# Half of the modulation product's weight loads on VectorE instead of TensorE, and a last tile finished bank by bank

## What is computed

```python
c_act = jax.nn.silu(c)                       # (1, 2048)
for l in range(2):
    mod = c_act @ w_mod[l] + b_mod[l]        # w_mod[l]: (2048, 6144)
    shift, scale, gate = jnp.split(mod, 3, axis=-1)
    h = rmsnorm(x, norm_gain[l]) * (1.0 + scale[:, None, :]) + shift[:, None, :]
    proj = h @ w_in[l]
    ...                                      # attention, retention: y
    x = x + gate[:, None, :] * (y @ w_out[l])
...
# PEER, for each token t: 8 heads x 16 chosen experts
a = gelu(einsum('thkd,td->thk', u[idx], hb))
out = einsum('thk,thkd->td', g * a, v[idx])  # added to the residual, then stored
```

## Time and profile before

| | us |
|---|---|
| median of 3 runs | 3162.84 (3162.42 to 3167.22) |
| the profiled execution's own time | 3161.82 |
| its span, first to last instruction | 3159.6 |
| PE busy (share of the span) | 2164.9 (69%) |
| DVE busy | 1692.1 (54%) |
| ACT busy | 853.3 (27%) |
| DMA, mean rate | 285 GB/s |

### The profile page before, as it was taken

How to read it: one execution, slowest core, us unless ns; L and a number is a source line. 1 busy time by engine, 2 the same in 40 slices (tenths; PEclk the granted TensorE clock), 3 DMA queues, 4 the chain that set the end, 5 groups by cost and what they waited for, 6 DMA issues and landing times.

```text
span 3159.6 us, 30717 instructions
## 1 busy us (share of the span) xinstructions
PE 2164.9 (69%) x12338; PEld 1487.2 (47%) x12338; DVE 1692.1 (54%) x2583; ACT 853.3 (27%) x1267; POOL 806.4 (26%) x680
## 2 busy tenths in 40 slices
PE   5899999989999999999989973223222222322335
PEld 2666677877778787667668872000000000000001
DVE  3436556654756664343335688665565555565430
ACT  1333443443444454454545421000000000000000
POOL 1111100000000000000000026665555555555552
PEclk8999999999999999999989987665666666666667
DMA  9888865557665555343325689999999999999998
GB/s 385 285 294 271 287 213 153 181 166 243 207 190 157 152 178 158 116 134 106 107 86 162 207 323 406 422 422 421 422 421 422 421 422 420 422 421 422 421 422 338
DMA packets 243593, 901.00 MB, mean 285 GB/s; under 512 B 20374, under 2 KB 45228, under 8 KB 177004
## 3 DMA queue, kind: packets, MB, share of 16 engines
q0 software_dynamic: 94208, 612.85, 48.3%
q1 hardware_dynamic: 148768, 285.58, 27.9%
q10 hardware_dynamic: 476, 0.62, 0.1%
HBM read 894.78 MB, written 2.10 MB: 284 GB/s over the span
## 4 chain that ended last, share of the span: by engine, by line
PE 56%; DMA 30%; DVE 7%; ACT 3%; issue 2%; POOL 2%; SPq 0%; DVEq 0%; ACTq 0%; POOLq 0%
PE pp L1786 48%; DMA late<-in_peer_v,MI 9%; PE tp L1786 6%; DMA P<-in_peer_v,MI 5%; DMA x<-in_peer_v,MI 5%; DMA ring<-in_peer_v,MI 4%; DMA SY<-in_peer_v,MI 2%; DVE wL L1112 2%; PE tp L1789 2%; DMA late<-in_w_mod 2%; ACT wH L613 1%; DMA ring<-in_peer_w_query 1%; POOL late L2319 1%; DMA ring<-in_w_in 1%; DMA P<-in_w_mod 0%
## 5 line engine op out<-in xcount | busy, mean ns | idle before, releaser
L1112 DVE TENSOR_TENSOR wL<-ring,wH 128x1024 fp32r<-128x1024 f32 (+3 forms) x504 | 583.8, 1162 | 765.0 <-ACT wH L613 763.7
L1786 PE MATMUL pp<-wH,hH 128*128 128x512 f32 (+3 forms) x1888 | 747.8, 396 | 16.2 <-issue 7.9
L613 ACT ACTIVATE wH<-ring 128x1024 fp32r<-128x1024 f32 (+3 forms) x504 | 508.0, 1010 | 784.8 <-PE pp L1786 650.8
L1786 PE MATMUL pp<-wH,hL 128*128 128x512 f32 (+3 forms) x1888 | 718.3, 380 | 0.0
L1786 PE MATMUL pp<-wL,hH 128*128 128x512 f32 (+3 forms) x1888 | 717.7, 380 | 0.0
L1786 PE MATMUL pp<-late,S 128*32 128x512 f32 x768 | 234.5, 892 | 336.9 <-DMA x<-in_peer_v,MI 157.9
L1786 PEld LDWEIGHTS pp<-wH,hH 128*128 128x128 f32 x1888 | 360.0, 191 | 159.5 <-issue 90.6
L1786 PEld LDWEIGHTS pp<-wH,hL 128*128 128x128 f32 x1888 | 359.2, 190 | 63.6
L1786 PEld LDWEIGHTS pp<-wL,hH 128*128 128x128 f32 x1888 | 360.8, 191 | 56.1 <-issue 1.0
L1745 DVE CUSTOM_DVE_ANT_0 late<-late,P 128x2048 f32<-128x2048 f32 x84 | 191.3, 2288 | 154.0 <-DMA late<-in_peer_u,MI 153.8
L1786 PE MATMUL pp<-P,S 128*32 128x512 f32 x360 | 157.8, 873 | 166.8 <-DMA late<-in_peer_v,MI 91.4
(11 more groups left out here) (303 smaller groups left out, 2925.5 us busy)
## 6 DMA issues: line engine op xcount, KB each, us to landing
ring<-in_w_in SPq DMA_DIRECT2D x288, 512.0 KB, 4.0
ring<-in_w_out SPq DMA_DIRECT2D x96, 512.0 KB, 4.4
P<-in_w_mod POOLq DMA_DIRECT2D x85, 512.0 KB, 4.9
late<-in_w_mod SPq DMA_DIRECT2D x64, 512.0 KB, 9.4
SY<-in_w_mod POOLq DMA_DIRECT2D x43, 512.0 KB, 5.1
ring<-in_w_in SPq DMA_DIRECT2D x48, 368.0 KB, 4.6
ring<-in_peer_w_query SPq DMA_DIRECT2D x32, 512.0 KB, 7.2
ring<-in_w_in SPq DMA_DIRECT2D x24, 344.0 KB, 3.2
```

What stands on the lines that cost most here:

```text
L613: act(heads(wH[k % NB][:, 0:2 * wd], 2), raw, ACT.Copy).then_inc(*tick("act_hi", ("hi", k)))
L1112: tt(lo, raw, hi.bitcast(F32), ALU.subtract).then_inc(*tick("dve_lo", *names))
L1786: return e.matmul(o, l, r, start=start, stop=stop, skip_group_check=skip)
```

## The change

From block 4 on, only the even k of a block are taken by PE. For the odd k, DVE multiplies the load by the column of `cact` and sums it into an accumulator of 128 x 1024 in four parts (`mod_acc`: 512 columns in hM, 256 in msum, 256 in U) with three instructions: 512, 256 and 256 columns. After k = 15, in a lane step of its own, PE waits for DVE's sums and adds the accumulator over its partitions with four more matmuls, whose weights are ones. A block has 17 lane steps instead of 16. The loads, their three buffers and their issuer stay as they were, but an odd load's buffer is now freed by DVE.

At the end of a token tile each bank has its own mark (`summed`), DVE adds a bank when that bank is done, and SP and ACT store its 512 columns with two DMAs each: 16 DMAs of 32 rows x 512 columns on either queue in the whole program, where SP had 8 of 32 x 2048.

```diff
@@ sync, add; scalar has the same with (2, 3), "out_act_done"
+            def store_rows(t, parts, sem):
+                for d in range(4):
+                    w.wait_ge(*at("added", t, d))
+                    for q in parts:
+                        e.dma_start(rows_d[t, 32 * q:32 * q + 32, d * 512:(d + 1) * 512],
+                                    xP[q:128:4, t, d * 512:(d + 1) * 512]).then_inc(*landed(sem, ("out", t, d, q)))
...
-                    w.wait_ge(*at("added", t, 3))
-                    for q in range(4):
-                        e.dma_start(rows_d[t, 32 * q:32 * q + 32, :], P[q:128:4, 0, t * D:(t + 1) * D]).then_inc(
-                            *landed("out_done", ("out", t, q)))
+                    store_rows(t, (0, 1), "out_done")
@@ scalar, store
-                                w.wait_ge(*at("mod used", 191 if p else 159))
+                                for m in (189, 190, 191) if p else (157, 158, 159):
+                                    w.wait_ge(*at("mod used", m))
@@ vector, mods
                     for k in range(16):
-                        if k < 15:
+                        if block >= 4 and k % 2:
+                            m = 16 * block + k
+                            w.wait_ge(*at("mod", m))
+                            w.wait_ge(*now("dve_side"))
+                            if k == 1 and block > 4:
+                                w.wait_ge(*at("side", block - 1))
+                            for o, acc in ((0, mod_acc_01), (512, mod_acc[2]), (768, mod_acc[3])):
+                                wv = mod_in[mod_slot(m)[0]][:, o:o + acc.shape[1]]
+                                names = [("mod used", m)] + ([("mod sums", block)] if k == 15 else []) if o == 768 else []
+                                if k == 1:
+                                    ts(acc, wv, cact[:, k:k + 1], None, ALU.mult, None).then_inc(*tick("dve_side", *names))
+                                else:
+                                    stt(acc, wv, cact[:, k:k + 1], acc, ALU.mult, ALU.add).then_inc(*tick("dve_side", *names))
+                        if k < 15 or block >= 4:
                             yield
@@ vector, add
-                    w.wait_ge(*at("mixed", 4 * t + 3, 7))
                     for d in range(4):
+                        w.wait_ge(*at("summed", t, d))
                         v = xP[:, t, d * 512:(d + 1) * 512]
                         tt(v, v, pp[d][:, :], ALU.add).then_inc(*tick("dve_h", ("added", t, d)))
@@ tensor, mods
-                        w.wait_ge(*at("mod", m))
+                        if block < 4 or k % 2 == 0:
+                            w.wait_ge(*at("mod", m))
+                            for g in range(4):
+                                z = mm(side_bank[32 * g:32 * g + 32, 0:256], cact[:, k:k + 1].to_broadcast([128, 32]),
+                                       wv[:, 256 * g:256 * g + 256], k == 0, k == 15)
+                            z.then_inc(*tick("pe_side", ("mod used", m), *([("side", n)] if k == 15 else [])))
+                        if k < 15 or block >= 4:
+                            yield
+                    if block >= 4:
+                        w.wait_ge(*at("mod sums", block))
                         for g in range(4):
...
+                            z = mm(side_bank[32 * g:32 * g + 32, 0:256], ones[:, 0:32], mod_acc[g], False, True)
+                        z.then_inc(*tick("pe_side", ("side", n)))
```

More of the change, by code:

```diff
@@ L422, in mixer_peer_program @@
                      "dve_lo", "dve_stored", "dve_x", "dve_y", "dve_h", "dve_side",
-                     *[f"mod_in{i}" for i in range(11)], "const_in", "pos_in", "x_in", "meta_in", "forget_in", "ffn_in", "decay_in", "turned_in", "out_done",
+                     *[f"mod_in{i}" for i in range(11)], "const_in", "pos_in", "x_in", "meta_in", "forget_in", "ffn_in", "decay_in", "turned_in", "out_done", "out_act_done",
                      *[f"ring_in{i}" for i in range(NS)], *[f"expert_in{i}" for i in range(NG)]):
@@ L456, in mixer_peer_program @@
                   SY[:, 1536:2560]]
+        mod_acc_01 = hM.rearrange("p k n -> p (k n)")
+        mod_acc = mod_acc_01[:, 0:256], mod_acc_01[:, 256:512], msum[:, 256:512], U[:, 3840:4096]
         bf, bf_s = sm[:, 72:80], sm[:, 80:88]
@@ L566, in mods @@
                             *landed(f"mod_in{b}", ("mod", m)))
-                for m in range(16 * b0, 16 * b1):
+                for m in range(16 * b0, 16 * b1 + (b1 - b0 if b0 else 0)):
                     yield
@@ L597, in sync, with store_rows @@
                     lanes.drain(*a)
-            w.wait_ge(*at("out", 1, 3))
+            w.wait_ge(*at("out", 1, 3, 1))
+            w.wait_ge(*at("out", 1, 3, 3))
         def scalar(e, w):
             act = e.activation
+            def store_rows(t, parts, sem):
+                for d in range(4):
+                    w.wait_ge(*at("added", t, d))
+                    for q in parts:
+                        e.dma_start(rows_d[t, 32 * q:32 * q + 32, d * 512:(d + 1) * 512],
+                                    xP[q:128:4, t, d * 512:(d + 1) * 512]).then_inc(*landed(sem, ("out", t, d, q)))
             turn, side, loads, cut = itertools.count(), itertools.count(), itertools.count(), itertools.count()
@@ L1068, in scalar @@
                     act(sc[i % 2], tp[u % 2][:, 0:512], ACT.Copy, scale=rsd[:, 4 + i // 4:5 + i // 4]).then_inc(*tick("act_h", ("pair free", u), ("scores", i)))
+                elif what == "add":
+                    store_rows(a[0], (2, 3), "out_act_done")
                 elif what == "gelu":
@@ L1893, in mods @@
                                 w.wait_ge(*at("side out", n - 1))
-                        w.wait_ge(*at("mod", m))
-                        for g in range(4):
[L1896 to L1900, removed]
+                        if block < 4 or k % 2 == 0:
[4 more added lines that the diff above has]
+                            z.then_inc(*tick("pe_side", ("mod used", m), *([("side", n)] if k == 15 else [])))
+                        if k < 15 or block >= 4:
+                            yield
+                    if block >= 4:
+                        w.wait_ge(*at("mod sums", block))
+                        for g in range(4):
+                            z = mm(side_bank[32 * g:32 * g + 32, 0:256], ones[:, 0:32], mod_acc[g], False, True)
+                        z.then_inc(*tick("pe_side", ("side", n)))
                     yield
@@ L2290, in tensor @@
                             if d == 3:
-                                m.then_inc(*tick("pe_piece", ("expert used", n), *([("mixed", i, b)] if c == 3 else [])))
+                                m.then_inc(*tick("pe_piece", ("expert used", n), *([("mixed", i, b)] if c == 3 else []),
+                                                 *([("summed", i // 4, d)] if final and c == 3 else [])))
+                            elif final and c == 3:
+                                m.then_inc(*tick("pe_piece", ("summed", i // 4, d)))
                 elif what == "open":
@@ L2341, in mods @@
                     yield
+                    if b0 and m % 16 == 15:
+                        yield
             def meta_sum(p, n):
```

## The result

| | before | after |
|---|---|---|
| median, us | 3162.84 (3162.42 to 3167.22) | 3185.6 (3177.06 to 3191.49) |
| ratio, 95% interval | | 1.0069 (1.0056 to 1.0082) |
| profiled execution's own time | 3161.8 | 3184.4 |
| span | 3159.6 | 3182.5 |

What follows compares the result with a forecast made beforehand. PE was taken to bind from 124 to about 950 us, the gathers from 1800 us on; -28.9 - 10.9 + 14.4 + 34 + 5 - 2.5 = +11.1 us gave 3173 us, forecast 3164 to 3184, range 3147 to 3190.

Steps and rivals of the forecast that it cites:

- the walk: Place-by-place count over 48 odd loads in blocks 4 to 9, carrying every wait on; PE waits at 18 even loads, 37 us.
- the loads land later: Rival: loads land in 5.5 us or more, buffer waits cost 41 us and all clock falls come, 14; 3189 us, chance 0.12.
- blocks 10 and 11: Second layer's projection: 32 places with loads on PE become 18, -10.9 us, with 0 for waits.
- Part 1: PE's matmuls on odd loads go: -28.9 us in blocks 4 to 9; DVE's three instructions take 1.42 us per load.
- Part 2: At a block's end PE waits for DVE before summing over partitions: +14.4 us for six blocks.
- Part 3: Blocks 4 to 9: DVE frees odd loads' buffers later, so PE waits for later loads, +34 us.
- the loads land sooner: Rival: loads land in the minimum 4.0 us, buffer waits cost 24 us and the clock 1; 3159 us, chance 0.24.
- the buffers don't bind: Rival: DVE's lag shrinks or later loads run ahead, no waits for loads; -27.9 us, 3134 us, chance 0.16.
- Part 4: PE's clock falls after long waits: three of eight waits over 2.5 us, about 1.7 us each, +5 us (0 to 14).
- Part 5: Program's end: three adds hide under PE's last matmuls, the last stores take 0.6 us more; -2.5 us (-4 to -1).

Runs made afterwards that it cites:

- e1_tail: The kernel before with only the bank-by-bank end, all loads of `w_mod` staying on PE; 3160.22 us against 3162.96, ratio 0.999.
- e3_early: The changed kernel with DVE taking odd load k+1 in the lane step of the even k, one step earlier; 3135.39 us, ratio 0.9917 to the kernel before.
- e6_later: The changed kernel with DVE taking each odd load one lane step later; 3285.88 us, ratio 1.0394 to the kernel before.
- e5_short: The changed kernel with DVE's three instructions cut to one of 8 columns for k >= 3; 3157.42 us against 3159.66 before, ratio 0.9999.
- e7_five: The changed kernel with five buffers for loads 64 to 111, three from 112 on; 3163.63 us, ratio 1.001 to the kernel before.
- e4_token: The kernel before with the bank-by-bank end, PE taking odd loads (k below 15) with one 8-column matmul, DVE none; 3137.36 us, ratio 0.9926.
- e2_late: The kernel before with DVE's odd loads in blocks 10 and 11 alone, and the bank-by-bank end; 3152.97 us, ratio 0.9968.
- e9_early_first: The changed kernel with DVE's odd loads one step earlier and lane M ahead of X and Y; 3137.45 us against 3162.73 before, ratio 0.9913.
- e8_early_five: The changed kernel with DVE's odd loads one step earlier and five buffers for loads 64 to 111; 3138.94 us, ratio 0.9937 to the kernel before.
- e10_first: The changed kernel with lane M ahead of lanes X and Y at each place; 3173.5 us, ratio 1.0038 to the kernel before.

## Why the prediction came out right, and where its terms were off

Predicted were 3173 us, slower, in 3147 to 3190; measured 3185.6. The direction and the mechanism held: in the changed trace PE waits most for even loads whose buffers DVE frees, and the two longest waits for loads, 5.04 us (load 84) and 4.95 (load 154), are at the two loads that the walk had named. The size is another matter. Measured is +22.8 us where +11.1 was forecast; the result is inside the range, but just past the forecast's own 3164 to 3184. Of the rival "the loads land later" one half came true, that all the clock falls come, and not the other, its landing time. (The sum, set on the median instead of the profiled execution, would have been 3174.) Term by term:

| term | predicted | measured |
|---|---|---|
| PE's matmuls in blocks 4 to 9 | -28.9 | -24; -28 with what else moved |
| sums at the blocks' ends | +14.4 | +13.5 |
| loads' buffers | +34 | +32.4 |
| clock | +5 | +13 |
| blocks 10 and 11 | -10.9 | -6 to -8.5 |
| the end | -2.5 | -0.8 in this profile, -2.8 in e1_tail's |

**Part 1, PE's matmuls: right to a few us.** From the offsets, 31.3 = 13.5 + 32.4 + 13.1 + rest gives -27.7 for the rest. Of that, 1.6 us is from pieces 1 to 8, which the change doesn't touch, and 1.6 from other waits of PE; the one of 3.82 us for the index keys is still there, with 4.14 us. What PE does outside the pieces, from piece 9 to the end of piece 104, took 63.0 us where it took 87.3, so the matmuls gave 24: loads taken at the lower clock cost more (1.08 us for the x8 at 186.62, against 0.64 in the earlier trace rows). The wait for the index keys in the changed kernel:

```profile
210.27 1.11 PE L1819 MATMUL tp<-CW,S 128*128 128x128 f32 x4 [4.14 <-DVE S L1345]
```

DVE's three instructions, 1.42 us predicted, begin at 133.02, and the next split begins at 134.47; the last of the three ends at 134.55:

```profile
133.02 0.74 DVE L1286 SCALAR_TENSOR_TENSOR hM<-P,cact,hM 128x512 f32<-128x512 f32 x1
...
134.08 0.47 DVE L1286 SCALAR_TENSOR_TENSOR U<-P,cact,U 128x256 f32<-128x256 f32 x1
134.47 0.91 DVE L1129 TENSOR_TENSOR wL<-ring,wH 128x736 fp32r<-128x736 f32 x1
134.85 0.53 POOL L2368 DMA_DIRECT2D P<-in_w_mod  x1 [4.23 <-DVE U L1286]
```

That is 1.53 us, and the issue follows 0.30 behind it, where the walk had 0.15 (its own row has 0.33 behind PE).

**Part 2, the sums: right.** The six waits of blocks 4 to 9 are 1.4, 1.2, about 0, 3.9, 3.3 and 3.5 us, predicted from 1.5 at block 4 to 3.2 at block 9. The longest, at block 7:

```profile
359.98 0.48 DVE L1286 SCALAR_TENSOR_TENSOR U<-P,cact,U 128x256 f32<-128x256 f32 x1
...
360.51 0.64 PE L1816 MATMUL pp<-hM,CW 128*32 128x256 f32 x2 [3.92 <-DVE U L1286]
```

**Part 3, the buffers: right in size and cause.** PE waits 36.5 us for loads where it waited 4.1. e3_early and e6_later show that the place is the cause, e5_short splits it into place and duration, e7_five removes it with buffers. That the size came out within 2 us has some luck in it: DVE's 1.53 + 0.30 us were 0.26 us more than the walk's 1.42 + 0.15, and the landings of the loads that PE waits for, the even ones from 68 to 158, took 4.5 us in the median, 0.4 less than its 4.9. The two errors work against each other. (Even and odd loads into P together took 5.1 in the median, 4.0 at least, 7.4 at most, at 158 to 474 us.)

Not in the walk was POOL's order. At 26 places up to load 158 the odd load went out right behind the even one, within 0.6 us (at 8 in the kernel before): its buffer had come free, but the even load ahead of it in POOL's queue was waiting for DVE. "Only these loads and four small ones stand on it" was true, but these loads hold up each other. It cost nothing that the trace shows: DVE never waits for a load in the changed kernel, and the even loads with an odd one right behind landed no later than the others (4.3 against 4.8 us in the median). In block 4 the even loads did land late, 6.1 us in the median (66 to 78) against 5.3 before.

The rival "the loads land sooner" would have needed 4.0 us. It was half right: the even loads landed in 4.5 us where they had taken 5.0 before. The Trainium skill (DMA: Bandwidth & Descriptors, Anatomy of one DMA — SWDGE (gpsimd) path) gives an estimate of 3.2 us; the trace doesn't agree, its shortest landing is 3.8, and with 3.2 the sum would have had the wrong sign. The rival "the buffers don't bind" fell too: waiting does let DVE catch up, but not enough.

**Part 4, the clock: the step that was mis-sized.** I counted waits over 2.5 us, took three of eight, and gave 1.7 us for each. The table sets two things side by side for each kernel, both from the first matmul of piece 9 to the last of piece 104: the time at which the granted clock shows the lower level, and the length of the pieces, each from its own first to last matmul, without what lies between them. Inside the pieces no trace shows any idle time of PE.

| kernel | at the lower level, us | pieces 9 to 104, us |
|---|---|---|
| before | 3.4 | 267.4 |
| e4_token | 3.4 | 268.0 |
| e1_tail | 10.2 | 269.1 |
| e2_late | 10.2 | 268.9 |
| e3_early | 20.5 | 270.6 |
| e9_early_first | 20.5 | 270.8 |
| e8_early_five | 23.9 | 270.0 |
| e5_short | 30.7 | 276.5 |
| e7_five | 41.0 | 276.1 |
| e10_first | 47.8 | 278.7 |
| after | 47.8 | 280.5 |
| e6_later | 146.8 | 304.1 |

The changed kernel shows the lower level (1.2 GHz) in ten stretches of 3.4 or 6.8 us (from about 161, 185, 199, 209, 260, 328, 359, 431, 475 and 502 us on). The kernel before has one in the same pieces (198, at the wait for the index keys, which the changed kernel has at 209). That is 44 us more, 33 of them inside pieces, and the pieces are 13.1 us longer: 0.30 us for each us, or 13.1 / 9 = 1.5 for each further fall. e6_later gives (304.1 - 267.4) / (146.8 - 3.4) = 0.26, the others from e1_tail on 0.13 to 0.33. So the price of 1.7 us was about right and the count was not. The waits over 2.5 us of parts 2 and 3 were eight, as counted, and behind or in every one of them the clock fell, where I took three; the ninth further fall is at 260, beside a wait of 1.78 us. With all eight, 14, the upper bound of the term, the forecast would have been 3182. The Trainium skill (TensorE: Matmul & The Clock Gate, Part 1: The HAM clock gate) has the rule, that an idle PE falls to half rate; the trace agrees, and the sum by the rule alone was the nearer one. It isn't so for every wait of that length: in e3_early none of its low stretches lies at a wait of 3.04 us that ends at 181.70. That the table is cause and not only company rests on the distance between matmuls, 0.21 us against 0.12 (184 to 192 us above); no run changes the clock alone.

**Blocks 10 and 11.** The price of a step was right (a step of one load against none: 1.22 - 0.45 = 0.77 us, predicted 0.78). "0" for the waits was not: in e2_late DVE's splits hold PE for 2.8 us and the low stretch at 759 us lasts 6.8 us, where e1_tail has 3.4. From piece 160 to piece 252 the changed kernel gains 8.5 us on the kernel before and e2_late 5.9; by the medians e2_late has 7.2 us over e1_tail.

**Part 5, the end.** Three adds hide under the matmuls, as predicted. The tail of the changed kernel, and of e1_tail, each with the durations of its DMA issues (ns min/median/max, first and last start):

```profile
3170.72 5.34 PE L1816 MATMUL pp<-late,S 128*32 128x512 f32 x32 [4.55 <-DMA late<-in_peer_v,MI]
...
3176.18 0.69 DVE L1801 TENSOR_TENSOR P<-P,pp 128x512 f32<-128x512 f32 x1 [0.23 <-PE pp L1816]
...
L555 SPq DMA_DIRECT2D out<-P x8: 469/592/2332, 3172.6 to 3179.5; - x8
L616 ACTq DMA_DIRECT2D out<-P x8: 499/852/2062, 3172.6 to 3179.5; - x8
```

```profile
3150.64 6.46 PE L1816 MATMUL pp<-late,S 128*32 128x512 f32 x32 [3.59 <-DMA late<-in_peer_v,MI]
...
L555 SPq DMA_DIRECT2D out<-P x8: 468/570/602, 3153.3 to 3158.6; - x8
L616 ACTq DMA_DIRECT2D out<-P x8: 499/614/866, 3153.4 to 3158.8; - x8
```

From PE's last matmul to the end of the span: 7.2 us before, 6.4 after (3176.06 to 3182.5), 4.4 in e1_tail (3157.10 to 3161.5). On SP an issue took the 0.6 us that I had from the earlier trace rows, on ACT 0.5 to 0.87. The queues keep up with the adds: the last bank's first issues start 0.25 us behind the end of the last add in the changed kernel (3177.12 and 3177.40, behind 3176.87). But there these two took 2.33 and 2.06 us, which is most of the 2 us by which the changed kernel's end is longer than e1_tail's; why they did, the trace doesn't show. The matmuls' own speed differs as well (5.34 against 6.46 us), so the two profiles show a range and no better number. The reading of ACT's order was off as well: what stands behind the stores of tile 0 is not free of a table load, one of 1.28 us (at 2593.34 before, at 2620.33 behind the stores in the changed kernel). From the end of piece 472 to the end of the span the changed kernel is still 1.7 us shorter than the kernel before, so nothing shows that it cost time.

## What to carry to other kernels

When work moves to an engine that writes nothing PE needs at once, ask where in that engine's order it frees its *input buffer*: here one lane step earlier turned +0.7% into -0.8%, and one step later into +3.9%. Put the slower engine's share ahead of the faster one's, by as much as its order lags, before adding buffers. If loads freed by two engines share one in-order issuer, the late one holds up the other; here that happened 26 times, and no wait came of it. Waits of 2 to 5 us scattered through a PE-bound stretch cost more than their own length, here about a quarter more (13 us on 46), because the granted clock fell at most of them.

## What the runs showed of the hardware that was not expected

- The granted clock fell in ten places of the changed kernel at 124 to 530 us, each time for 3.4 or 6.8 us: at all nine waits of PE over 2.5 us (2.88 us ending at 159.41, 5.04 at 186.62, 3.92 at 200.13, 4.14 at 210.27, 3.13 at 328.23, 3.92 at 360.51, 3.30 at 429.52, 4.95 at 475.13, 3.52 at 500.74), and at 260 behind one of 1.78. Eight shorter waits, of 1.2 to 2.42 us, had none. A us at the lower level made the pieces 0.30 us longer, not 0.5: a part of it falls into the wait itself, as at 184 to 188 us, and into work between the pieces.
- A DMA issue of 32 rows x 512 columns took as long on SP as one of 32 rows x 2048 columns, 0.6 us in the median, and up to 0.87 on ACT with both issuing at once; two in one profile took over 2 us.
- A scalar_tensor_tensor of 512 float32 columns took 744 ns on data from SBUF alone, against 685 ns for the one that reads PSUM.
- Filling the DMA queues further gave no time: 385 instead of 364 GB/s at 124 to 160 us (e8_early_five, e3_early) bought shorter waits for `w_mod`, and the projection's own loads took 8.5 us to land instead of 5.9, with one wait of PE of 10.3 us where e3_early has 4.2.
